# Output projections of a two-layer encoder in three fp32r passes, with the experts' first weight loads behind them

## The reference

```python
# SEQ 512, D_MODEL 1024, DEPTH 2; everything float32
def reference(x, c, ...):
    for i in range(DEPTH):
        sh1, sc1, g1, sh2, sc2, g2 = ada(c, i)
        h = rms_norm(x) * (1.0 + sc1) + sh1
        if i % N_MIXERS == 0:
            y = gdn_mixer(h, ...)        # gated delta rule, 8 heads of 128
        else:
            y = fox_mixer(h, ...)        # forgetting attention, 16 heads of 64
        x = x + g1 * y
        h = rms_norm(x) * (1.0 + sc2) + sh2
        x = x + g2 * hier_moe(h, ...)    # 4 groups of 8 experts, top 1 group, top 2 experts
    return rms_norm(x, final_norm)

# both mixers end in the product that the change is about:
    return o.reshape(B, L, GDN_DIM) @ w_out        # gdn, 512x1024 @ 1024x1024
    return o @ w_out                               # fox, 512x1024 @ 1024x1024
```

## Time and profile before

| | us |
|---|---|
| median of 3 runs | 1465.35 |
| lowest, highest | 1463.05, 1469.11 |
| profiled execution: time | 1467.78 |
| profiled execution: span | 1466.2 |
| mean granted TensorE clock | 0.96 of full |
| PE busy | 1337.1 |
| DVE, ACT, POOL busy | 731.8, 435.3, 397.0 |

### The profile page before, as it was taken

The page is one execution under the profiler, slowest core; times in us unless marked ns, Lnnn a source line. Parts: engine busy times, 40 slices in busy tenths (PEclk is TensorE's granted clock), DMA queues, the critical chain, the costliest instruction groups (busy, mean ns, idle before and its releaser), DMA issues.

```text
span 1466.2 us, 24949 instructions
## 1 busy us (share of the span) xinstructions
PE 1337.1 (91%) x9111; PEld 859.8 (59%) x9111; DVE 731.8 (50%) x1520; ACT 435.3 (30%) x1033; POOL 397.0 (27%) x588
## 2 busy tenths in 40 slices
PE   4999999999999989999886999999999979999881
PEld 2677767777775455555442777777764545555440
DVE  3656566667652466522223445666654557322224
ACT  4434424434442110000002645555541200000002
POOL 3022022112230023444334054434410024344320
PEclk8899999999999989999898899999999999999996
DMA  8255554512154279999997222122046379999995
GB/s 360 115 208 201 215 213 177 197 59 115 58 222 131 114 263 405 418 418 419 421 420 319 90 88 73 73 80 108 26 191 239 154 277 415 421 419 418 419 398 200
DMA packets 56693, 350.27 MB, mean 239 GB/s; under 512 B 18408, under 2 KB 18880, under 8 KB 30992
## 3 DMA queue, kind: packets, MB, share of 16 engines
q1 hardware_dynamic: 44992, 332.02, 57.1%
q0 software_dynamic: 11520, 16.83, 3.1%
q10 hardware_dynamic: 80, 0.04, 0.0%
HBM read 342.45 MB, written 27.34 MB: 252 GB/s over the span
## 4 chain that ended last, share of the span: by engine, by line
PE 70%; DMA 15%; DVE 9%; issue 2%; ACT 2%; POOL 1%; SPq 0%; POOLq 0%; DVEq 0%; ACTq 0%
PE PS L1116 10%; PE PS L771 8%; DMA hT<-in_moe_w_down_dram 8%; PE PS L773 7%; PE PS L772 7%; PE PS L1059 6%; PE PS L1123 5%; DMA Dr<-in_ada_w_dram 4%; PE PS L749 2%; PE PS L1143 2%; PE PS L1133 2%; PE PS L862 2%; PE PS L908 2%; PE PS L1108 2%; PE PS L1294 2%
## 5 line engine op out<-in xcount | busy, mean ns | idle before, releaser
L771 PE MATMUL PS<-hHi,Whi 128*128 128x512 f32 x512 | 225.3, 440 | 2.5 <-DVE hLo L1789 2.4
L773 PE MATMUL PS<-hHi,Wlo 128*128 128x512 f32 x512 | 202.8, 396 | 0.0
L772 PE MATMUL PS<-hLo,Whi 128*128 128x512 f32 x512 | 202.0, 394 | 0.0
L1360 ACT COPY arena<-PS 128x512 f32<-128x512 f32 (+4 forms) x256 | 108.6, 440 | 281.9 <-PE PS L862 104.7
L1116 PE MATMUL PS<-Wr,arena 128*64 128x256 f32 x1408 | 165.4, 389 | 9.8 <-DVE arena L2195 9.8
L1583 ACT ACTIVATE arena<-PS 128x128 f32<-128x128 f32 x72 | 20.0, 278 | 464.9 <-PE PS L1116 369.0
L1116 PEld LDWEIGHTS PS<-Wr,arena 128*64 128x64 f32 x1408 | 101.5, 140 | 88.8 <-issue 29.0
L2477 POOL DMA_INDIRECT y_rows<-arena x72 | 77.0, 1070 | 258.5 <-DVE arena L2207 252.2
L2418 POOL TENSOR_TENSOR Wlo<-Wr,Whi (+1 forms) x72 | 94.0, 1324 | 178.7 <-ACT Whi L1360 178.7
L771 PEld LDWEIGHTS PS<-hHi,Whi 128*128 128x128 f32 x512 | 97.6, 191 | 33.8 <-issue 18.2
L2201 DVE TENSOR_TENSOR arena<-arena,PS 128x128 f32<-128x128 f32 x72 | 20.7, 288 | 185.6 <-ACT arena L1583 169.0
(11 more groups left out here) (394 smaller groups left out, 2301.6 us busy)
## 6 DMA issues: line engine op xcount, KB each, us to landing
Wr<-in_moe_w_gate_up_dram SPq DMA_DIRECT2D x52, 2048.0 KB
Dr<-in_ada_w_dram SPq DMA_DIRECT2D x42, 1024.0 KB, 26.8
Dr<-in_moe_w_down_dram SPq DMA_DIRECT2D x28, 1024.0 KB
arena<-in_moe_w_gate_up_dram SPq DMA_DIRECT2D x14, 2048.0 KB
hT<-in_moe_w_down_dram SPq DMA_DIRECT2D x26, 1024.0 KB
Wr<-in_gdn_w_dram SPq DMA_DIRECT2D x8, 2048.0 KB, 8.6
Wr<-in_fox_w_dram SPq DMA_DIRECT2D x8, 2048.0 KB, 8.1
shift_scale<-in_moe_w_down_dram SPq DMA_DIRECT2D x12, 1024.0 KB
```

The source lines that it names most:

```text
L771: mm(out_ap, a_hi, b_hi, start=(k == 0), stop=False)
L772: mm(out_ap, a_hi, b_lo, start=False, stop=False)
L773: return mm(out_ap, a_lo, b_hi, start=False, stop=(k == KD - 1))
L1360: return nc.scalar.copy(dst, src)
```

## The change

1. `out_part` and `out_projection` call `out_product`, which is `mm3` over `OThi`, `OTlo`, `Whi`, `Wlo`. `OTlo` lies over `OT`, `OThi` over `hLo` (that is, over `hT`).
2. The two output halves become an eighth and a ninth section: ACT casts them in the last two steps (the last two calls get `w_n` 5), DVE (layer 0) or POOL (layer 1) makes the low halves.
3. `mixed_hi` on ACT and `mixed_lo` on DVE split `OT` row by row, inside the last step where the tables `MIXED` and `MIXED_FOX` say, the eighth row behind it.
4. The 14 filler products begin later (`late` 13 of 32 in layer 0, 16 of 32 in layer 1).
5. Gate-up loads of experts 0 and 4 no longer go ahead of the projection, since `Whi` is in use. 0 and 1 go once the first four units are done, 2 after the last unit, 3 and 4 after the last `h_rows` store. `up_rows` is reordered to (0, 2, None, 1, 3), and at the end of layer 0 section 1 is loaded ahead of section 0.
6. The transposed rows of the experts' phase lie in the arena (`routed`), and POOL's clearing of `xg` waits for `r_ps` in place of `wo_ps`.

```diff
+MIXED = ((), (0,), (1, 2), (3,), (4, 5), (6,), ())
+MIXED_FOX = ((0, 1, 2), (3, 4), (5, 6), ())
...
+        OTlo = sb_over(arena_at, "OTlo", [P, KD, T])
+        OThi = hLo
...
-        up_rows = [arena[:, 0:KD * T] if u is None else Wr[:, u].rearrange("p k n -> p (k n)") for u in (3, 1, None, 0, 2)]
+        up_rows = [arena[:, 0:KD * T] if u is None else Wr[:, u].rearrange("p k n -> p (k n)") for u in (0, 2, None, 1, 3)]
...
-                for e in (0, 4)[:2 if layer else 1]:
-                    expert_load(layer, e, e)
-
...
-                    expert_load(0, 4, 4)
...
                 sp.wait_ge(wo_ps, i * 2 * NT + NT)
-                expert_load(i, 3, 3)
+                for e in range(2):
+                    expert_load(i, e, e)
...
                     if n == 1:
                         sp.wait_ge(wo_ps, (i + 1) * 2 * NT)
-                        expert_load(i, 1, 1)
                         expert_load(i, 2, 2)
+                for e in (3, 4):
+                    expert_load(i, e, e)
...
-                    for p in range(2):
-                        sp.wait_ge(m["gu_ps"], max(ENDS[q] for q in ((28, 29), (30, 31))[p]) + 1)
+                    for p in (1, 0):
+                        sp.wait_ge(m["gu_ps"], max(ENDS[q] for q in ((30, 31), (28, 29))[p]) + 1)
...
-            def out_part(layer, w_sem, ready, fills):
+            def out_part(layer, late, fills):
...
                 def fill(a, b):
-                    for f in range(2 * (KD - 1) * a // fills, 2 * (KD - 1) * b // fills):
+                    n = 2 * (KD - 1)
+                    for f in range(n * max(a - late, 0) // (fills - late), n * max(b - late, 0) // (fills - late)):
...
-                        mm(PS[u][:], tile(OT[:, k, :], u), Wr[:, 0, k, :], start=(k == 0), stop=False)
+                        if u == 0:
+                            pe.wait_ge(h_lo, (2 * layer + 1) * KD + k + 1)
+                        out_product(u, 0, u, k)
...
+            def out_product(bank, nh, n, k):
+
+                return mm3(PS[bank][:], tile(OThi[:, k, :], n), tile(OTlo[:, k, :], n), Whi[:, nh * KD + k, :], Wlo[:, nh * KD + k, :], k)
...
-                            last = mm(PS[u % 2][:], tile(OT[:, k, :], n), Wr[:, nh, k, :], start=(k == 0), stop=(k == KD - 1))
+                            last = out_product(u % 2, nh, n, k)
...
+            def mixed_hi(layer, ks):
+
+                for k in ks:
+                    act.wait_ge((proj_ps, fpj_ps)[layer], 4 * H)
+                    act.wait_ge((ot_ok, on_ok)[layer], k + 1)
+                    cp(OThi[:, k, :], OT[:, k, :]).then_inc(h_hi, 1)
...
-            step(7, 1)
-            delta(7, None, lambda m: None, 1)
+            step(7, 1, 5)
+            delta(7, None, lambda m: None, 1, 5)
             head_norm(7)
+            mixed_hi(0, (7,))
...
+                    if mixed:
+                        mixed_hi(1, MIXED_FOX[qt])
                     if w_n is not None:
                         weights_hi(par, (2 * qt,))
...
-            pair_step(7, 1)
-            attend(7, lambda m: None, 1)
+            pair_step(7, 1, 5)
+            attend(7, lambda m: None, 1, 5, mixed=True)
+            mixed_hi(1, (7,))
...
+            def mixed_lo(layer, ks):
+
+                for k in ks:
+                    dve.wait_ge(h_hi, (2 * layer + 1) * KD + k + 1)
+                    TT(OTlo[:, k, :], OT[:, k, :], OThi[:, k, :], ALU.subtract).then_inc(h_lo, 1)
...
             for p in range(H - 2, H):
-                attend(p, split=False)
+                attend(p)
```

More of the change, by code:

```diff
@@ L351, in build, with turned_of @@
         Y = [arena[:, a:a + NT * D].rearrange("p (n d) -> p n d", n=NT) for a in (0, 8 * D)]
+        routed = arena[:, 7680:7680 + KD * T].rearrange("p (k t) -> p k t", k=KD)
+        def turned_of(phase):
+            return routed if phase % 2 else hT
         def half_of(ap, l, which):
@@ L734, in narrow @@
                     for k in range(KD):
-                        last = mm(PS[6][:, n * width:(n + 1) * width], tile(hT[:, k, :], n), w[:, k, :],
+                        last = mm(PS[6][:, n * width:(n + 1) * width], tile(turned_of(phase)[:, k, :], n), w[:, k, :],
                                   start=(k == 0), stop=(k == KD - 1))
@@ L1040, in _, with out_projection @@
             step(7, 1)
-            delta(H - 1, out_part(0, mix_w, ot_ok, 4 * KD), 1, more=False)
-            def out_projection(layer, w_sem, ready, ready_n):
+            delta(H - 1, out_part(0, 13, 4 * KD), 1, more=False)
+            def out_projection(layer):
                 pe.wait_ge(modq_in, 32 * (layer + 1))
@@ L2346, in attend @@
                         square_low(p + 1, qt - 2)
+                    if not more:
+                        mixed_lo(1, MIXED_FOX[qt])
                 dve.wait_ge(fev, p * 4 + 4)
@@ L2361, in _ @@
             attend(H - 1, more=False)
+            mixed_lo(1, (H - 1,))
             out_projection(1)
```

48 lines of the change are left out of this document (28 added, 20 removed).

## The result

| | before | after |
|---|---|---|
| median of the runs, us | 1467.23 (4 runs) | 1489.78 (4 runs, 1483.75 to 1491.50) |
| profiled execution: time / span, us | 1467.78 / 1466.2 | 1491.0 / 1489.1 |
| mean granted clock | 0.960 | 0.948 |

The ratio is 1.0135 (95% interval 1.010 to 1.017): slower by 1.35%. Run again later in six more executions (a_again) it was 1.0148 (1.0108 to 1.0188), median 1486.67. The ratios are those on record and not quotients of the medians shown; the two differ by up to 0.25% (a_again: 1.0123 by the medians). The forecast was 1472.8, with a range up to 1481.

The account below looks back on a forecast made before the run. PE was taken as the bound, except memory in the two expert phases. Profiled 1467.8 - 6.0 (layer 0) + 3.0 (between layers) + 10.4 (layer 1) = 1475.2; carried to the median, 1465.35 + 7.4 = 1472.8 us, range 1460 to 1481.

Parts of the forecast that it names:

- The sign: Whole kernel against no change: slower 0.45, same 0.44, faster 0.11.
- The saving: Projections, units 2 to 7: 48 products, each 0.176 us cheaper at 0.68 us, 8.4 us less per layer.
- The hand-over: Last row of OT to first projection product: an added ACT cast and DVE subtraction, plus 1.4 us per layer.
- Layer 0's last head: Step 7 of layer 0: subtractions nearly fit DVE's free time, filler moves late; plus 1.0 us (bounds 0 and 3).
- The expert loads: Start of each expert phase: 2.1 MB more behind the last unit still fits the DMA gap; cost 0 (bounds 0 and 3).
- Rival C: Expert phases: late gate-up sets not hidden, saturated phase moves up to 5 us per layer, 1480 in all; chance 0.15.
- Between the layers: Turn to layer 1: POOL's later subtractions lie over the first four expert sums on DVE; plus 3.0 us (bounds 0 and 4.1).
- Pair 6: Layer 1: exponentials wait 8.4 us for output half 0, then half clock costs 2.0; together 10.4 us (bounds 7 and 12).
- Pair 7: Layer 1: landing, casts and crowded filler 4.5 us, POOL's subtractions 0.5, clock 2; together 7.0 us (bounds 3 and 11).

Follow-up runs that it names:

- e_turn: Changed kernel plus dummy products in layer 0's last step, and first five gate-up sets in other slots so layer 1's section 0 loads first: 1481.90 us, ratio 1.0115.
- b_late0: Kernel before, with only layer 0's 14 plain f32 filler products begun later, from position 13 of 32; no casts or splits: 1474.06 us, ratio 1.0039.
- e_early: Changed kernel with the load of output half 0 put ahead of the mask rows of pair 7: 1472.23 us, ratio 1.0035.
- c_base: Changed kernel with five dummy products in layer 0's last step and output half 0 loaded ahead of pair 7's mask rows: 1473.86 us, ratio 1.0048.

## Why the prediction was wrong

The sign was on the side that I gave 0.45, and the size was not: 1489.8 lies 9 us over the range. By its steps:

- **The saving**: right. Units 2 to 7 and what is behind them took 8.0 us less from the first product to the routing's end (8.4 forecast); a product costs 0.70 us and not 0.68.
- **The hand-over**: right. From the row of `OT` to the first product 2.17 us instead of 0.75, plus 1.4.
- **Layer 0's last head**: the step that failed, by the term "plus 1.0 us (bounds 0 and 3)". It measured 2.1 us where the clock held, within the bounds, 3.3 in a_again and 8.6 in the profiled execution of the result, where it fell for 16 us. I had used the clock in pairs 6 and 7 from the earlier trace rows and had seen that the filler "now covers ACT's copy no longer in the first levels", but did not carry the one to the other: I looked for time that DVE and ACT need, and the thing lost was PE's activity. This is 7.6 us of the miss in the profiled execution; what it is in the median stays open.
- **The expert loads**: failed by the term "cost 0 (bounds 0 and 3)", which measured 4.6 us in layer 0 and 1.9 in layer 1. I asked whether the traffic fits into the gap, and it does. I did not ask what a late gather does to the first item. In layer 0 PE idles for 2.9 us instead of 1.2 and begins it at 0.50, the item takes 2.3 us more, and all the streaming hangs on its end. In layer 1 the item was slow before as well, and the rows that came 2.1 us later are all of it. Part of the 4.6 is the luck of the profiled execution of before, whose item in layer 0 ran at full clock. Rival C had the size (5 to 10 us for both layers) with another mechanism, a set that is waited for. It was not that one.
- **Between the layers**: right in direction and size, 2.6 against 3.0, less surely in mechanism. The sums are slowed as foreseen, but the eighth ends only 1.5 us later; e_turn takes this back, and the executions differ by as much again with the clock.
- **Pair 6**: right in mechanism and near in size, 11.6 against 10.4: the landing took 9.2 us and not 8.0. The 8.0 was that of half 1; half 0 stands behind the mask rows, issued 0.4 us ahead of it, and the same load took 9.05 us in b_late0, which has the order of before. e_early takes all of the 11.6 back.
- **Pair 7**: right in the sum, 7.0, less in its parts. I gave 4.5 to landing, casts and crowded filler together, 0.5 to the subtractions and 2 to the clock. Against c_base the repair of landing, casts and subtractions brought 1.1 and the dummies 1.2, neither clear of the spread, and two filler products moved brought 2.5. The rest of the 8 us that the pair costs in c_base stays open, so the right sum is in part luck.
- The remainder, 1.0 us in pairs 0 to 5 and 1.0 in the last experts, has the size by which executions of one kernel differ in a stretch, and was not looked into.

The failed terms miss by 7.6 and 6.5 us, 14.1 of the 15.5 between forecast and result in the profiled execution (+7.4 and +22.9). The median of a_again, 1486.67, is over the range too. In layer 0 both are of one kind: idle time of PE that was added a few us ahead of a stretch that PE's speed decides. The range was drawn from the bounds of the terms, and these held no clock in the two places where I saw no stall.

## What to carry to other kernels

Filler on the tensor engine does two things: it does its own work, and it keeps the clock. An edit that makes it cheaper or later needs an upper bound with the stretch behind the new idle time at half speed, and dummies at the old places are the cheap test of it (0.3 us here). One profiled execution can't tell what such a stretch costs: the same code took 45.7 us in one and 52.2 in another. A new wait at the head of an engine's loop was cured where the transfer is issued (11.6 us for one load moved ahead of another), and work moved onto GpSimd can land on the small VectorE operations beside it (8.58 us for eight of 0.16).
